# Two modulation tiles moved from ahead of the expert loop into the attention, and unread products in TensorE's waits

## The reference, cut to what matters

```python
def ada_mod(c, w, b):
    m = jax.nn.silu(c) @ w + b
    return jnp.split(m[:, None, :], 6, axis=-1)
...
for layer in range(DEPTH_2):
    shift_m, scale_m, gate_m, shift_f, scale_f, gate_f = ada_mod(c, ada_w[layer], ada_b[layer])
    h = modulate(rms_norm(x, norm_gains[layer, 0]), shift_m, scale_m)
    j = layer // 2
    if layer % 2 == 0:
        y = attn_hybrid_mixer(h, att_w_qkv[j], att_w_o[j], pos)
    else:
        y = retention_mixer(h, ret_w_in[j], ret_gn[j], ret_w_o[j], pos)
    x = x + gate_m * y
    h = modulate(rms_norm(x, norm_gains[layer, 1]), shift_f, scale_f)
    x = x + gate_f * swiglu(h, ffn_w_gate_up[layer], ffn_w_down[layer])
return rms_norm(x, final_norm)
```

## Time and profile before

| | us |
|---|---|
| runs | 2100.84, 2105.84, 2100.69 (median 2100.84) |
| profiled execution | 2105.16, its span 2103.4 |
| mean granted clock of TensorE | 0.993 |
| TensorE busy | 2020.8 (96%) |
| DVE busy | 1127.3 (54%) |
| ACT busy | 706.6 (34%) |
| chain that ended last | TensorE 73%, DMA 21%, DVE 4% |
| DMA in the expert loop's slices | 427 to 429 GB/s |

### The profile page before, as it was taken

One profiled execution on the slowest core, in us unless ns is written; L12 is line 12 of the kernel. 1 busy time (PEld: TensorE's weight loads), 2 busy tenths in 40 slices (PEclk: granted clock), 3 DMA queues, 4 the chain that ended last, 5 costly groups with the idle time before them and its releaser, 6 DMA issues.

```text
span 2103.4 us, 28445 instructions
## 1 busy us (share of the span) xinstructions
PE 2020.8 (96%) x11488; PEld 1337.7 (64%) x11488; DVE 1127.3 (54%) x1735; ACT 706.6 (34%) x932; POOL 3.1 (0%) x10
## 2 busy tenths in 40 slices
PE   7999999999999999999999999899999999998998
PEld 7999998853333333333333333298888898887887
DVE  6998888642222222221222212368788686656764
ACT  4334555411111111111111111175555453544543
POOL 0000000000000000000000000000000000000000
PEclk9999999989999999999999999999999999999999
DMA  9554759999999999999999999963397765555752
GB/s 339 188 175 167 280 212 363 369 372 393 427 427 427 427 428 428 428 428 429 429 428 429 429 429 429 414 225 115 131 309 247 263 230 177 201 191 174 235 175 85
DMA packets 188011, 654.91 MB, mean 311 GB/s; under 512 B 10992, under 2 KB 76528, under 8 KB 162704
## 3 DMA queue, kind: packets, MB, share of 16 engines
q1 hardware_dynamic: 187920, 653.59, 79.9%
HBM read 652.50 MB, written 1.06 MB: 311 GB/s over the span
## 4 chain that ended last, share of the span: by engine, by line
PE 73%; DMA 21%; DVE 4%; ACT 1%; issue 1%; SPq 0%; DVEq 0%; ACTq 0%
DMA ring<-w_down 19%; PE front L1019 19%; PE front L1070 14%; PE front L1316 11%; PE pair L1344 7%; PE front L1040 5%; PE pair L1040 2%; PE front L977 2%; PE front L1042 2%; PE pair L1384 2%; PE pair L1296 1%; PE pair L1042 1%; PE front L1326 1%; DMA ring<-ada_w 1%; DVE ring_low L2296 1%
## 5 line engine op out<-in xcount | busy, mean ns | idle before, releaser
L2296 DVE TENSOR_TENSOR ring_low<-ring,w_high 128x2048 fp32r<-128x2048 f32 (+1 forms) x179 | 404.2, 2264 | 141.9 <-ACT w_high L1693 141.3
L1316 PE MATMUL front<-ring,arena 128*64 128x512 f32 x1808 | 403.2, 595 | 9.7 <-DMA ring<-w_gu 9.6
L1693 ACT ACTIVATE w_high<-ring 128x2048 fp32r<-128x2048 f32 (+1 forms) x179 | 338.1, 1893 | 189.5 <-PE front L1070 78.1
L1019 PE MATMUL front<-x_parts,w_high 128*128 128x256 f32 x2048 | 373.5, 285 | 11.2 <-DVE ring_low L2496 9.3
L2792 DVE TENSOR_TENSOR arena<-front,par 128x512 f32<-128x512 f32 x64 | 43.9, 686 | 623.4 <-PE front L1326 623.4
L1019 PEld LDWEIGHTS front<-x_parts,w_high 128*128 128x128 f32 x2048 | 321.0, 193 | 15.0 <-issue 11.9
L1316 PEld LDWEIGHTS front<-ring,arena 128*64 128x64 f32 x1808 | 125.8, 137 | 277.8 <-issue 244.3
L1019 PE MATMUL front<-x_parts,ring_low 128*128 128x256 f32 x1024 | 290.5, 284 | 0.0
L1070 PE MATMUL front<-w_high,arena_r 128*128 128x512 f32 x736 | 229.4, 390 | 1.3 <-DVE ring_low L2296 0.7
L1344 PE MATMUL pair<-ring,arena 128*64 128x512 f32 x864 | 195.1, 597 | 26.7 <-DMA ring<-w_down 26.7
L1019 PEld LDWEIGHTS front<-x_parts,ring_low 128*128 128x128 f32 x1024 | 197.2, 193 | 0.0
(11 more groups left out here) (364 smaller groups left out, 2351.5 us busy)
## 6 DMA issues: line engine op xcount, KB each, us to landing
ring<-w_gu SPq DMA_DIRECT2D x113, 2048.0 KB, 23.6
ring<-w_down SPq DMA_DIRECT2D x57, 2048.0 KB, 25.4
ring<-ffn_w_gate_up SPq DMA_DIRECT2D x44, 1024.0 KB, 7.8
ring<-ada_w SPq DMA_DIRECT2D x20, 2048.0 KB, 8.6
ring<-ret_w_in SPq DMA_DIRECT2D x12, 2048.0 KB, 7.9
ring<-w_in SPq DMA_DIRECT2D x10, 2048.0 KB, 8.0
arena<-w_gu SPq DMA_DIRECT2D x10, 2048.0 KB, 13.3
ring<-ffn_w_down SPq DMA_DIRECT2D x8, 2048.0 KB, 8.5
```

The source lines that it names most:

```text
L1019: mm = pe.matmul(acc_bank[:, ch * T:(ch + 1) * T], w[:, k, ch * P:(ch + 1) * P], xs[:, kk, :], start=kk + ch + n == 0, stop=kk == b.kc - 1 ...
L1316: mm = pe.matmul(bank[b][64 * o:64 * o + 64, :], xgT[:, k // 4, k % 4, :], gu_cols(b_in, j, D * o + 512 * b), start=k == 0, stop=k == DC - 1)
L1693: nc.scalar.activation(high_part(u), raw_part(u), ACT.Copy).then_inc(sem("w_high"), 1)
L2296: V.tensor_tensor(low_part(u), raw_part(u), high_part(u).bitcast(F32), ALU.subtract).then_inc(sem("w_low"), 1)
```

## The change

Tiles 10 and 11, the gate of layer 0's feed-forward, are no longer in set 0. They are loaded in the attention, one ahead of the block aq[1] and one behind it, and DVE sums them there in four parts of four steps. The `ada_rows` of these two gets a place of its own behind block 3 of layer 0's gate and up, and the later ones are numbered one higher. The write of this gate's row moves from the attention to the load of the first tile of down[0][1], its read to the next tile. In layer 1's feed-forward four of the sum's steps move from ahead of block 4 to just behind block 0, so that tile 22's eight stand together. Ahead of the loop the products of tiles 10 and 11 go, and the expert tiles are loaded in another order of places, with one wait fewer. Products that nothing reads (`fill`, 128x128 by 256 columns) are added: four after the logits, two ahead of gather(0), one ahead of the wait for its result, and twelve behind the last scatter.

```diff
@@ -51,11 +51,11 @@
 BIAS_ROUND = 6
-ADA_SETS = (range(0, 12), range(12, 16), range(16, 20), range(20, 22), range(22, 24))
+ADA_SETS = (range(0, 10), range(10, 16), range(16, 20), range(20, 22), range(22, 24))
+ADA_PASSES = ((10, 14, 1), (14, 16, 1), (16, 20, 2), (20, 22, 3), (22, 24, 4))
 ADA_SUMS = 8
...
 SUMMED, LENT = (2, 3, 4, 5, 7), (2, 4, 5)
-PARTED = 10
 SUM_ROWS = ((2, 3, 4, 5), (7,))
@@ -294,7 +294,7 @@
             for _ in range(n):
-                if len(ada) in LENT or len(ada) == PARTED:
+                if len(ada) in LENT:
                     ada.append(None)
@@ -366,7 +366,6 @@
         plan.stop()
-        ada_tiles(2)
         turn_2 = plan.turn()
@@ -382,7 +381,9 @@
         av.append(plan.block([(qkv_w, 2 * D, 512)], token=True))
+        ada_tiles(1)
         aq.append(plan.block([(qkv_w, 512, 512)]))
+        ada_tiles(1)
         ak.append(plan.block([(qkv_w, D + 512, 512)]))
@@ -641,7 +642,6 @@
         cv_flat = cv_pad[:, :, :].rearrange("p c t -> p (c t)")
-        parted = (big(1), big(3))
         early_sums = [cv_flat[:, RH * T:RH * T + COLS], cv_flat[:, RH * T + COLS:RH * T + 2 * COLS], ada_acc,
@@ -861,20 +861,15 @@
             sp.wait_ge(sem("x_out"), XHEADS)
-            for k, home in enumerate(parted):
-                c0 = 512 * PARTED + HALF * k
-                sp.dma_start(home, a["ada_w_2"][0][:, c0:c0 + HALF].rearrange("(k p) n -> p k n", p=P)).then_inc(
-                    sem("lent_in"), 16)
+            slot_tile(first_slots[0])
+            slot_tile(first_slots[2])
             slot_tile(first_slots[1])
-            slot_tile(first_slots[0])
             sp.wait_ge(sem("mm_done"), xo[1].units[0].done)
             first_tile(RING)
-            slot_tile(first_slots[2])
+            slot_tile(first_slots[3])
             split_tile(1)
             sp.wait_ge(sem("tok_ready"), TT * (t_2.n + 1))
-            sp.wait_ge(sem("ada_product"), products_of(PARTED + 1))
             first_tile(FRONT)
-            slot_tile(first_slots[3])
             sp.wait_ge(sem("h_tok"), TT)
@@ -922,9 +917,12 @@
                     write_gate(0)
+                if t.n == N1 + RING + 2:
+                    read_gate(0, 1)
+                if t.n == down[0][1].units[0].tile.n:
+                    sp.wait_ge(sem("ada_in"), 1)
                     write_gate(1)
-                if t.n == N1 + RING + 2:
-                    read_gate(0, 2)
+                if t.n == down[0][1].units[0].tile.n + 1:
                     read_gate(1, 2)
@@ -1104,17 +1102,10 @@
                 j, last = i - ADA_SETS[s].start, i == ADA_SETS[s].stop - 1
-                if i != PARTED:
-                    arrived(ada[i])
+                arrived(ada[i])
                 for k in chunks:
...
                     shifted = silu_c[:, at_col:at_col + 32]
-                    if i == PARTED:
-                        for h, home in enumerate(parted):
-                            pe.wait_ge(sem("lent_in"), 16 * len(LENT) + 32)
-                            mm = pe.matmul(ada_bank[s][o:o + 32, HALF * h:HALF * (h + 1)], shifted, home[:, k, :],
-                                           start=False, stop=False, skip_group_check=True)
-                        continue
                     mm = pe.matmul(ada_bank[s][o:o + 32, :], shifted, at(ada[i])[:, k, :],
@@ -1132,14 +1123,15 @@
                 pe.wait_ge(sem("consts_set"), 5)
-                i = ADA_SETS[h + 1]
-                pe.wait_ge(sem("ada_sum"), DC * (i.stop - ADA_SETS[1].start))
-                if h:
-                    pe.wait_ge(sem("ada_in"), h)
+                first, stop, s = ADA_PASSES[h]
+                pe.wait_ge(sem("ada_sum"), DC * (stop - ADA_SETS[1].start))
+                if s > 1:
+                    pe.wait_ge(sem("ada_in"), s - 1)
                 for q in range(4):
-                    at_col, m = ADA_SUMS - 1 - q, i.start + q % len(i) - ADA_SETS[1].start
-                    mm = pe.matmul(ada_bank[h + 1][32 * q:32 * q + 32, :], ones_at[:, at_col:at_col + 32], ada_sums[:, m % 4, :],
-                                   start=True, stop=True, skip_group_check=True)
+                    i = first + q % (stop - first)
+                    at_col, m = ADA_SUMS - 1 - (first - ADA_SETS[s].start + q), i - ADA_SETS[1].start
+                    mm = pe.matmul(ada_bank[s][32 * q:32 * q + 32, :], ones_at[:, at_col:at_col + 32], ada_sums[:, m % 4, :],
+                                   start=first == ADA_SETS[s].start, stop=stop == ADA_SETS[s].stop, skip_group_check=True)
                 mm.then_inc(sem("ada_row"), 1)
@@ -1261,8 +1253,12 @@
             token(xo[1], s_attn)
-            ada_product(10)
             turn(t_2)
+
+            def fill(dst, n, columns):
+
+                for _ in range(n):
+                    pe.matmul(dst[:, 0:columns], ident, c1[:, 0:columns], start=True, stop=True)
 
@@ -1276,7 +1272,7 @@
             logits(1).then_inc(sem("r_logits"), 1)
-            ada_product(11)
+            fill(bank[0], 4, T)
             pe.wait_ge(sem("r_mask"), 1)
@@ -1397,9 +1393,11 @@
 
+            fill(bank[0], 2, T)
             gather(0, True)
...
             turn_inputs(0)
+            fill(bank[0], 1, T)
             pe.wait_ge(sem("m_xgT"), 1)
@@ -1442,6 +1440,7 @@
             scatter(rest + 1, True)
+            fill(bank[3], 12, T)
 
@@ -1597,8 +1596,10 @@
                         feature(b, s_h[2 * layer + 1], turned=None if i else ("h1", "h3")[layer])
+                    if layer == 0 and i == 3:
+                        ada_rows(0)
                     if i == 7:
-                        ada_rows((0, 3)[layer])
+                        ada_rows((1, 4)[layer])
                     if i == 8:
@@ -1609,7 +1610,7 @@
                 feature(b, s_h[2], turned="h2" if b is rq[0] else None)
-            ada_rows(1)
+            ada_rows(2)
 
@@ -1663,7 +1664,7 @@
                 ret_turned(h)
-            ada_rows(2)
+            ada_rows(3)
             token(ro[0], ret_split, ("ret_split", 0, 4), units=(0,))
@@ -1832,7 +1833,7 @@
                 if s:
-                    act.wait_ge(sem("ada_row"), s)
+                    act.wait_ge(sem("ada_row"), s + 1)
                 else:
@@ -2884,7 +2885,8 @@
                         if m >= 4:
-                            dve.wait_ge(sem("ada_row"), m // 4)
+                            before = [first <= ADA_SETS[1].start + m - 4 < stop for first, stop, _ in ADA_PASSES]
+                            dve.wait_ge(sem("ada_row"), before.index(True) + 1)
                         V.tensor_scalar(dst, w, c, None, ALU.mult).then_inc(sem("ada_sum"), 1)
@@ -2951,14 +2953,18 @@
             low_until(units_of(av[0])[0])
+            ada_sum(4)
             dve.wait_ge(sem("c2_in"), 32)
             low_until(units_of(av[0])[1])
+            ada_sum(4)
             sb_abs(0)
...
             low_until(units_of(aq[1])[0])
+            ada_sum(4)
             sb_abs(2)
...
             low_until(units_of(aq[1])[1])
+            ada_sum(4)
             for p in range(NSB // 2):
@@ -3002,7 +3008,7 @@
             resids = [TT]
-            gates_read = (2, 2, 3, 4)
+            gates_read = (1, 2, 3, 4)
 
@@ -3071,7 +3077,7 @@
                         scales(2)
-                    if layer == 0 and i or layer == 1 and 1 <= i <= 4:
+                    if layer == 0 and i or layer == 1 and 1 <= i <= 3:
                         ada_sum(4)
@@ -3086,7 +3092,7 @@
                                     ALU.subtract).then_inc(sem("ff_hidden"), 1)
-                    if layer == i == 0:
+                    if i == 0:
                         ada_sum(4)
...
                     low_until(units_of(down[layer][0])[2])

```

## The result

| | before | changed |
|---|---|---|
| median of 22 runs | 2101.28 | 2106.34 |
| lowest and highest | 2098.48, 2107.96 | 2102.77, 2109.01 |
| span of the profiled execution | 2103.4 | 2104.3 |

The ratio is 1.0019, with a 95% interval from 1.0013 to 1.0025: slower by 2.7 to 5.3 us, and by 5.1 as the medians have it. That is clear of the noise, but under the 0.3% from which I called it a difference. The forecast was 2105.4, which is +4.6. The two profiled executions differ by 0.9 us only, because that of before was one of its long runs (2105.16 against a median of 2101.28). I therefore ran the kernel before once more. Its second profile (2100.79, span 2099.0) is of the usual sort, and with it the spans differ by 5.3 us, as the medians do.

A forecast was written before the change was run, and what follows sets the result against it. Expert-weight transfers bound 848 to 1314 us; behind them TensorE with DVE set the end. Terms -0.4 + 5.2 + 1.0 + 5.8 - 7.8 = +3.8, with 0.8 for clock +4.6: 2100.84 became 2105.4, range 2092.0 to 2111.6.

The forecast's parts named there:

- the likeliest case: Whole kernel: the forecast's own case, 2105.4 us with range 2102 to 2109, chance 0.50.
- edit 1: Ahead of the loop: two tiles and two ada_product less gain 0; fills behind the last scatter give -0.4 us.
- edit 2: Attention: tile 11's load lands late behind the gate write and DVE waits, +5.2 us; bounds 0.8 and 6.3.
- edit 3: Layer 0's feed-forward: one ada_rows more, four products where TensorE has no idle, +1.0 us; bounds 0.6 to 1.2.
- edit 4: Layer 0's down projection: write_gate(1) makes the load behind it late and TensorE waits, +5.8 us; bounds 0 and +7.2.
- edit 5: Layer 1's gate and up: eight sum steps together free the slot earlier, the stall goes, -7.8 us; bounds -6.3 and -8.
- the 0.8 for the clock: Attention and layer 0's down projection: clock loss after TensorE's two new idles, 0.8 us for both together.
- upper end of the range: Whole kernel: 2111.6 us, with attention and down-projection terms at their upper ends and 3.5 us of clock each.
- The -0.4 behind the last scatter: Before the attention: if fills keep the clock, DVE's 0.46 us wait for the transposes goes; -0.4 us (0 to -0.5).
- Rival (a): Ahead of the loop: fills keep the clock, TensorE enters the loop 5.3 us earlier, 2100.1 us; chance 0.18.
- rival (b): Attention and layer 0's down projection: the write doesn't hold the queue, -6.4 us in all, 2094.4 us; chance 0.17.
- Rival (c): Attention and layer 0's down projection: TensorE's clock falls after each new idle, +8.8 us, 2109.6 us; chance 0.15.

The follow-up runs named there:

- b2: The kernel before, unchanged, run again for a second profile: 2100.79 us.
- e8: The kernel before with layer 1's four sum steps moved behind block 0 and fifteen unread products added: 2092.13 us, ratio 0.9962.
- e9: The kernel before with layer 1's sum move, gate 2 written behind ret_w_o's first tile, and fifteen unread products: 2091.52 us, ratio 0.9950.
- e5: The changed kernel with all gate rows written in 32-byte runs, 128 pieces instead of 1024: 2096.41 us, ratio 0.9977 to the kernel before.
- e10: The changed kernel with gates written in 32-byte runs and without its nineteen unread products: 2097.16 us, ratio 0.9973 to the kernel before.
- e1: The kernel before with only layer 1's four sum steps moved from ahead of block 4 to behind block 0: 2093.47 us, ratio 0.9955.
- e7: The kernel before with layer 1's sum move and gate 2 written behind the first tile of ret_w_o: 2092.64 us, ratio 0.9963.
- e3: The changed kernel with gate 1 written two loads earlier and its read one tile earlier: 2105.40 us, ratio 1.0015 to the kernel before.
- e6: The changed kernel with gates 0 and 1 written from ACT's DMA queue instead of SP's: 2105.52 us, ratio 1.0015 to the kernel before.
- e11: The changed kernel with gates written in 32-byte runs and four more unread products where ada_product(10) stood: 2095.54 us, ratio 0.9975 to the kernel before.
- e4: The changed kernel without its nineteen unread products: 2109.98 us, ratio 1.0036 to the kernel before.
- e2: The changed kernel with gate 0 written behind tile 10's load, near 1357 instead of 1384: 2100.55 us, ratio 0.9990 to the kernel before.

## Why the prediction was right, point by point

**The sum.** 2105.4 was forecast and 2106.34 measured, or +4.6 and +5.1, and the likeliest case, that each 4-byte write costs TensorE a stall and layer 1's stall goes, is the one that came. That the total is so near is partly luck. By the table and the points below the terms missed by +1.9 (edit 1), +1.1 (edit 2), +0.2 (edit 3), -1.7 (edit 4) and +0.1 (edit 5), and the 0.8 for the clock had no place of its own. The upper end of the range, 2111.6, is 2100.84 + 3.8 + 7.0; with edits 2 and 4 at their upper ends too, as the text says, it would be 2114.1.

**Edit 1** is the term that missed by most: -0.4 in all, and the table has +1.5. This number hangs on which two profiles are compared. In all fourteen profiles of these kernels the granted clock fell to 0.50 at some time from 433 to 443 us. How long it stayed there differs, and the longer it stayed the later the attention's transposes began: 3.4 us at half and a start at 1368.8 to 1370.3 (b2, e8, e9), 17.1 us and 1374.7 to 1375.0 (e5, e10). The kernels before, b2, e1 and e7 have the same instructions up to there, and the stretch at half was 3.4 to 13.6 us in them. The changed kernel, e3, e5 and e6 are the same up to there too, and have 6.8 to 17.1. At an equal stretch of 10.2 us the changed kernel began the attention at 1371.8, e1 at 1373.1 and e7 at 1372.9. So the instructions of edit 1 cost nothing that these profiles show, and the +1.5 is the clock's. The medians, less the table's other rows, leave some 1.2 us for this stretch (an estimate: 5.1 - 6.3 - 5.3 + 7.7). My forecast had put the clock's share at 0, because the waits of TensorE stayed where they were. Whether the half clock lasts longer because ada_product(10) is gone, or by chance, is open: seven of the eight kernels without it have 10.2 us or more, three of the six with it. Putting products back in that place did not shorten it (e11, 13.7 us). The -0.4 behind the last scatter came: from the end of the last w_down wait to the transposes the changed kernel took 59.4 us, 59.7 without the fills. Rival (a) is out: with and without fills the stretch was the same, 10.2 us in the changed kernel and e4, 17.1 in e5 and e10.

**Edit 2.** +5.2 forecast, +6.3 measured, at the upper of the bounds 0.8 and 6.3. (The lower one is 0.6 by its own terms: 1405.3 + 10.0 against 1414.72.) Landing 1408.9 against 1409.9, logs at 1418.72 against 1419.9; but all of it started 2.1 us earlier than in the profile that I reckoned from, and TensorE's idle was 6.0 us, not 5. The step that was short is the load's: it landed 8.6 us behind the write, not 7.6. e2 and e5 show that the write is the cause, 5.6 us of it.

**The mechanism of the hold** was named wrongly. I wrote that the write holds the queue and what is behind it starts when it has landed. That gave nearly the right times for loads behind the write. But e6 shows that a load of another queue is late too, and a load just ahead of a write can be late as well (13.2 instead of 7.0). So it is not SP's queue that is held, but something that both queues share. The estimate of 0.7 us behind rival (b) does not hold for this write, which took 16.0 and 16.1 us to land. It was worked out from a figure of the Trainium skill, "DMA: Bandwidth & Descriptors", section "Bandwidth", that is for transfers from DRAM to SBUF, in another direction than this one. The Trainium skill's statement on the same page, under "Rules for kernel authors", that a last dimension in single elements makes one descriptor of each, agrees with e5's count of packets.

**Edit 3.** +1.0; gate and up of layer 0, up to the first L1068 (1633.66) or L1070 (1628.35, first profile), took 127.5 us against 126.4, +1.2.

**Edit 4.** +5.8 forecast, some +4.1 measured (5.3 less 1.2). The stall came, at another tile: 3.1 us at the last tile of down[0][0], ahead of the write, and only 0.3 at the tile behind it. My term took that tile as in time and the one behind as 5.8 late. Since the first stall had already moved TensorE, the second was nearly hidden.

**Edit 5.** -7.8, measured -7.7, alone some -8 (e1).

**Rival (c)**, a clock lost behind each new idle, came in part. Behind the first idle, that of the attention, the changed kernel's clock fell to 0.50:

```profile
1420.00:1424.00 4.00, 2.51 (x8) 2.27 (x9) 3.90 (x6) 3.34 (x3) 0.00 (x0) 0.50 0.62 228
```

It cost almost nothing there: counted from the attention's start the logs were 6.1 us later than in the first profile of before, and the whole attention 6.3 us longer. Behind the second idle the changed kernel's clock kept 1.00 (1650 to 1670), and e4's did not (0.85 and 0.81). There layer 0's feed-forward took 199.6 us instead of 196.8, of which 1.4 us are the longer wait.

## What to carry to other kernels

Count the pieces of a small DMA, not its bytes: 4 KB in elements of 4 bytes took 16 us to land, made the load behind it late in the attention, the retention and both down projections, made the load just ahead of it late in some places, and did so from either queue. Write it in longer runs, or where no load is waited for within some 20 us. Before a difference of a few us is explained from two profiles, hold each against the median of its own runs: here one was 4 us long, and the sum came right only with a second one. Where the clock sets a stretch's length, two profiles are still too few: the same instructions differed there by 4 us. When a change is a bundle, run its parts: one edit here won 8 us, and the rest gave back 13.

## What the runs showed of the hardware that I had not expected

A 1.5 MB load issued 0.4 us ahead of a write of 1024 pieces landed in 13.2 us instead of 7.0. That effect on the load ahead is not steady. The same tile of ada_w landed in 13.4, 16.6 and 18.7 us in three executions of the same instructions, and in 12.8 and 12.9 with no write behind it. In the attention of the kernel before, the load 0.4 us ahead of two such writes landed in 8.1 us, no later than elsewhere. The slow time is also not the time in which the small packets are recorded: 1053 of them lie in one microsecond, and the loads behind them moved at 14 to 51 GB/s for 6 us more.
